# A fused two-model kernel: loads joined and reordered, products evicted in place in PSUM, norm heads reordered, and index products woven with half sweeps

## The chip, the cores and the metric

One core of one Trainium2 chip. The metric is device microseconds of the whole program; lower is better. Everything runs in one launch, with the loads of 250 MB of weights in it.

## What is computed

Two small transformer stacks of two layers each, on 512 tokens of width 1024, in float32, one after the other on the same `x`:

```python
# first_block, l = 0, 1
h = rms(x, norm_g[l]);  proj = h @ w_in[l]
y_a = gla(gq, gk, gv, decay) * silu(gz)                      # gated linear attention
score = sum_h w[t,h] * relu(iq[t,h] . ik[s])                  # 8 index heads of 64
y_b = softmax(q k^T over the top 128 keys of score) v * silu(bz)
y_c = differential attention * silu(cz)
x = x + (sigmoid(g0)*(y_a@w_br0) + sigmoid(g1)*(y_b@w_br1) + sigmoid(g2)*(y_c@w_br2)) @ w_out[l]
# second block, l = 0, 1
h = rms(x, norm1)*(1+scale1) + shift1;  x = x + gate1 * mixer(h @ w_in_2) @ w_out_2
h2 = rms(x, norm2)*(1+scale2) + shift2; x = x + gate2 * (relu(h2 @ w_ff1)**2 @ w_ff2)
```

## The kernel before, in words

**Arithmetic.** Every big product is made of three fp32r matmuls: weights and activations are each split into a high part (rounded to fp32r) and a low part (the rest), and high x high, high x low and low x high are added in PSUM. For a slab of weights `raw` of 128x1024 (two chunks of 128 rows, 512 columns) ScalarE writes the high part `wh` (`high(g)`, L1070), and GpSimd subtracts it from `raw` to give `wl` (L693). SyncE loads the slabs into a ring of `RING`=6 slots; `wh` has `SPLIT`=5. For activations, ScalarE writes `hTh` and VectorE `hTl`.

**The order.** `make_timeline` writes one list, `line`, of steps; every engine walks through that same list and does its own part of each step, in order, so a step's place in `line` is its place in each engine's queue. A *sweep* `(i, p, q)` is what TensorE does with slab q of unit i for a pair p of its four output slices: 2 slices x 2 chunks x 3 matmuls = 12 matmuls (L763). A unit of 1024 rows has 2 pairs x 4 slabs = 8 sweeps, one of 512 rows 4. After a pair's last slab each slice is evicted by `evacuate`, on ScalarE and on VectorE. SyncE and ScalarE do their loads and `high(g)` at the sweep steps, before the eviction; `high` waits both for the slab's DMA and for TensorE's release of the slot.

**PSUM.** Eight banks. Sweeps take banks 0 to 3 in turn (ring `proj`); index products, transposes and small products take 4, 5 and 6 (ring `aux`); a head's transposes take 4 to 7 (ring `turn`). TensorE waits, before it writes a bank, for the event `free` of the bank's last user.

**Scratch.** `scr` has four slots of 128x512, handed out in turn to eviction steps that need a temporary.

**A norm head** (`norm_head`, six of them: the opening, layer 1 of the first block, and two for each layer of the second) turns `x` into `hTh`/`hTl`, pair by pair of the four token tiles: `stats` (ScalarE, squares with a sum, L1184), `scale` (VectorE, a Newton root in 128x1 steps L1592/L1597, then `xn = x * root`, L1602), `turn` (TensorE transposes two half tiles of `xn`, L717; VectorE multiplies by the gain, L1612 or L1617, and adds the shift, L1619, in PSUM; ScalarE copies to `hTh`, L1191; VectorE subtracts to `hTl`, L1626). These steps are laid among the last four sweeps of the unit before and the first four of the unit after.

**The stages that the change touches besides.** The opening: `cf`, four tiles of `x`, twenty small rows (`COLS`), then six slabs, then the late constants in 20 more DMAs. The index stage: 32 products `iq . ik` (L822), four of them for each of the eight sweeps of unit `bk`; ScalarE takes the relu from PSUM to `scr` (L1212) and VectorE adds it, weighted, to `score` (L1668/L1671). The gated branches (`br`), the mixer's output (`mix`), the feed-forward units up (`fu`, L1448, L1450, L1149, L1453) and down (`fd`, L1463, and L1471, L1473, L1477 in the last group). `mod` steps (L1813) are 96 weighted sums of a second stream of weights on VectorE, spread evenly over a list of eligible sweeps; sweeps with a `stats` or `turn` within the next four steps are not eligible.

## Time and profile before

| | |
|---|---|
| runs | 2834.9, 2839.28, 2841.01 us; median 2839.28 |
| the profiled execution | 2836.87 us, of which the span on the core is 2834.8 us |
| TensorE matmul busy | 2523.5 us (89%) |
| VectorE / ScalarE / GpSimd busy | 1439.2 (51%) / 943.5 (33%) / 878.7 us (31%) |
| mean granted TensorE clock | 0.955 of full speed |
| HBM traffic | 249.6 MB read, 90 GB/s over the span |

The busy share of TensorE is that of the whole program. Its idle time is not spread evenly: it lies in the opening, around the norm heads, and in the attention stages, where small operations follow one another from engine to engine.

### The profile page before, as it was taken

To read this page: it belongs to the slowest core of one execution; us is meant where nothing else is said; L and a number is where in the kernel's file an instruction comes from. 1 tells how busy PE (TensorE), PEld (TensorE's weight loads), DVE (VectorE), ACT (ScalarE), POOL (GpSimd) and SP (SyncE) were. 2 spreads that over 40 slices of the span, in tenths; PEclk is the share of its full clock that TensorE was granted. 3 is DMA by queue.
4 is the path that set the end of the run, shared out by engine and by line. 5 is a ranking of instruction groups with operands and counts; after the bars stand their busy time and mean duration, and the time that the engine had idled before them with its cause. 6 is when DMAs were issued, how large, how long until landed. Compare 5 with 4: busy or idle time off the path is not lost. (4 is left out here: it accounts for less than half of the span.)

```text
span 2834.8 us, 34357 instructions
## 1 busy us (share of the span) xinstructions
PE 2523.5 (89%) x12303; PEld 2008.5 (71%) x12303; DVE 1439.2 (51%) x2993; ACT 943.5 (33%) x1695; POOL 878.7 (31%) x366
## 2 busy tenths in 40 slices
PE   5998999889999899989977878999997777899999
PEld 4676877677768677767776547878776644787877
DVE  4496243654368733365465456454556554623334
ACT  3433243432343224342233442322223354232221
POOL 2332314233324242323422002454442200244442
PEclk9999999999999999999998799999998889999999
DMA  4232414134323241313432002444433200233332
GB/s 140 88 90 67 148 39 134 45 97 164 126 65 90 90 141 54 110 58 106 162 88 64 1 1 60 141 162 142 147 121 83 64 1 1 60 95 99 95 96 77
DMA packets 133573, 256.01 MB, mean 90 GB/s; under 512 B 23382, under 2 KB 30116, under 8 KB 133412
## 3 DMA queue, kind: packets, MB, share of 16 engines
q1 hardware_dynamic: 133412, 253.83, 28.5%
q8 instruction: 105, 1.72, 0.2%
q14 instruction: 56, 0.46, 0.1%
HBM read 249.60 MB, written 4.19 MB: 90 GB/s over the span
## 5 line engine op out<-in xcount | busy, mean ns | idle before, releaser
L693 POOL TENSOR_TENSOR wl<-raw,wh 128x1024 fp32r<-128x1024 f32 (+2 forms) x362 | 878.5, 2431 | 1928.5 <-ACT wh L1070 1927.3
L763 PE MATMUL ps<-wh,hTh 128*128 128x512 f32 (+3 forms) x1600 | 645.6, 403 | 16.1 <-DVE hTl L1626 16.1
L1070 ACT ACTIVATE wh<-raw 128x1024 fp32r<-128x1024 f32 (+2 forms) x362 | 379.9, 1049 | 841.4 <-PE ps L763 440.9
L763 PE MATMUL ps<-wl,hTh 128*128 128x512 f32 (+3 forms) x1600 | 625.7, 391 | 0.0
L763 PE MATMUL ps<-wh,hTl 128*128 128x512 f32 (+3 forms) x1600 | 625.2, 391 | 0.0
L763 PEld LDWEIGHTS ps<-wh,hTh 128*128 128x128 f32 x1600 | 311.9, 195 | 86.2 <-issue 30.8
L763 PEld LDWEIGHTS ps<-wh,hTl 128*128 128x128 f32 x1600 | 310.6, 194 | 60.3
L763 PEld LDWEIGHTS ps<-wl,hTh 128*128 128x128 f32 x1600 | 312.1, 195 | 52.7
L763 PE MATMUL ps<-hTh,wh 128*128 128x512 f32 (+2 forms) x704 | 258.8, 368 | 4.9 <-DVE hTl L1626 3.7
L763 PE MATMUL ps<-hTh,wl 128*128 128x512 f32 (+2 forms) x704 | 257.8, 366 | 0.0
L763 PE MATMUL ps<-hTl,wh 128*128 128x512 f32 (+2 forms) x704 | 257.7, 366 | 0.0
L717 PE MATMUL ps<-cf,arena 128*128 128x128 f32 x800 | 133.5, 300 | 136.2 <-DVE arena L1982 23.7
L717 PEld LDWEIGHTS ps<-cf,arena 128*128 128x128 f32 x800 | 101.8, 154 | 175.9 <-issue 82.7
L1813 DVE SCALAR_TENSOR_TENSOR modw<-modw,cact 128x1024 f32<-128x1024 f32 x96 | 151.2, 1581 | 139.9 <-DMA modw<-in_w_mod_dram 139.1
L763 PE MATMUL ps<-wh,yTh 128*128 128x512 f32 x448 | 178.7, 399 | 9.9 <-DVE scr L1450 9.9
L763 PE MATMUL ps<-wl,yTh 128*128 128x512 f32 x448 | 176.0, 393 | 0.0
L763 PE MATMUL ps<-wh,yTl 128*128 128x512 f32 x448 | 175.7, 392 | 0.0
L763 PEld LDWEIGHTS ps<-hTh,wh 128*128 128x128 f32 (+1 forms) x704 | 132.7, 189 | 27.3 <-issue 6.1
L763 PEld LDWEIGHTS ps<-hTh,wl 128*128 128x128 f32 (+1 forms) x704 | 132.7, 189 | 21.3
L763 PEld LDWEIGHTS ps<-hTl,wh 128*128 128x128 f32 (+1 forms) x704 | 132.7, 188 | 21.3
L1448 DVE TENSOR_SCALAR scr<-ps 128x512 f32<-128x512 f32 (+1 forms) x72 | 45.1, 627 | 180.2 <-PE ps L763 180.2
L1463 DVE TENSOR_TENSOR arena<-ps,arena 128x512 f32<-128x512 f32 x96 | 66.3, 691 | 109.3 <-PE ps L763 108.3
(262 smaller groups left out, 3277.1 us busy)
## 6 DMA issues: line engine op xcount, KB each, us to landing
raw<-in_w_in_dram SPq DMA_DIRECT2D x160, 512.0 KB, 3.6
raw<-in_w_ff_dram SPq DMA_DIRECT2D x128, 512.0 KB, 3.7
modw<-in_w_mod_dram SPq DMA_DIRECT2D x96, 512.0 KB, 4.7
raw<-in_w_br_dram SPq DMA_DIRECT2D x24, 512.0 KB, 3.7
raw<-in_w_out_dram SPq DMA_DIRECT2D x24, 512.0 KB, 3.7
xm<-in_x_dram SPq DMA_DIRECT2D x8, 512.0 KB, 4.5
raw<-in_w_out_dram SPq DMA_DIRECT2D x16, 256.0 KB, 3.9
raw<-in_w_in_dram SPq DMA_DIRECT2D x8, 408.0 KB, 3.3
```

The source lines that it names most:

```text
L693: pool.tensor_tensor(piece(wl, g % RING, u), piece(raw, g % RING, u), piece(wh, g % SPLIT, u).bitcast(F32), ALU.subtract)\
L717: last = pe.transpose(dst[:, c * P:(c + 1) * P], src[:, c * P:(c + 1) * P], ident)
L763: last = pe.matmul(*args, start=(q == 0 and c == 0 and n_pass == 0), stop=(q == u["quarters"] - 1 and c == u["chunks"] - 1 and n_pass == 2))
L1070: act.activation(piece(wh, g % SPLIT, u), piece(raw, g % RING, u), ACT.Copy)\
L1448: dve.tensor_scalar(tmp, b, 0.0, None, ALU.max).then_inc(dve_result, mark(dve_result))
L1463: dve.tensor_tensor(acc, b, acc, ALU.add).then_inc(dve_result, mark(dve_result, free))
L1813: dve.scalar_tensor_tensor(w, w, 0.5, cact[:], ALU.mult, ALU.mult, accum_out=modT[:, m // MOD_STEPS, m % MOD_STEPS:m % MOD_STEPS + 1])\
```

## The change

It is a bundle. (1) The opening loads `x` tiles 0 and 1 with a semaphore of their own, then slabs 0 and 1, then `x` tiles 2 and 3, then all small rows as one DMA that the host has laid out, then the other slabs; the late constants are six DMAs. ScalarE makes no `high` before the first `stats`, and writes the opening's squares to `scr`. (2) In every head, ScalarE writes `xn` of the even tile (scale from `nsm[:,3,0:1]`), VectorE that of the odd tile; `stats(0)` and its `scale` stand ahead of the four last sweeps, not behind the first of them; VectorE and ScalarE treat the two tiles of a pair together, first half (`hb`=0) of both, then the second half of both. In the opening, `stats` of pair 1 stand ahead of the first transposes, and two sweeps, not one, ahead of the second ones. (3) `mix`, `br`, `fu`, `fd` and index evictions keep their temporary in the product's own PSUM bank. The bank is freed by the last of the operations. (4) The next-to-last feed-forward group adds the accumulator, scales and adds to `x`, so the last group has two operations a slice and not three. (5) The index stage lays half a sweep (one slice, step `front`, and then the sweep's other slice) behind every two index products, not a sweep behind every four. (6) `logit_max` scales by -q in one 128x1 `tensor_scalar` for each column, where it was one `scalar_tensor_tensor`.

The core of the diff:

```diff
+    def halved(fill):
+
+        return [x for step in fill for x in (("front", *step[1:]), step)]
+
...
-            line.extend(last[0:1] + stats(0) + last[1:3] + two("turn", 0) + last[3:4] + stats(1))
+            line.extend(stats(0) + last[0:3] + two("turn", 0) + last[3:4] + stats(1))
             line.extend(first[0:3] + two("turn", 1) + first[3:4] + then + first[4:])
         else:
-            line.extend(stats(0) + [("columns",)] + two("turn", 0) + stats(1))
-            line.extend(first[0:1] + two("turn", 1) + first[1:4] + [("constants",)] + then + first[4:])
+            line.extend(stats(0) + [("columns",)] + two("stats", 1) + two("turn", 0) + [("scale", stage, 1)])
+            line.extend(first[0:2] + two("turn", 1) + first[2:4] + [("constants",)] + then + first[4:])
 
     if 1 in blocks:
...
-            weave(idx, U("bk", C_BK, 512, tok()))
+            weave(idx, halved(U("bk", C_BK, 512, tok())))
...
+            first_stage = ("n", 0) if 1 in blocks else ("a", 0)
+            for pair, sem in enumerate((first_x_loaded, x_loaded)):
+                for t in (2 * pair, 2 * pair + 1):
+                    sp.dma_start(xm[:, t], a["x"][0, t * P:(t + 1) * P, :]).then_inc(sem, mark(sem, by=16))
+                for t in (2 * pair, 2 * pair + 1):
+                    note(("x", first_stage, t), sem)
+                if pair == 0:
+                    load_weights(0)
+                    load_weights(1)
+            sp.dma_start(rows[0:N_COLS, :], a["rows"]).then_inc(const_loaded, mark(const_loaded, "consts", by=16))
+
...
+                    sp.dma_start(rows3[0:96, :], a["rows_mod"]).then_inc(late_loaded, mark(late_loaded, by=16))
+                    sp.dma_start(rows2[0:64, :], a["rows_pe"]).then_inc(late_loaded, mark(late_loaded, by=16))
+                    sp.dma_start(glag.rearrange("p l n -> p (l n)"), a["gla_gains"].partition_broadcast(P))\
+                        .then_inc(late_loaded, mark(late_loaded, by=16))
+                    sp.dma_start(lqk.rearrange("p k n -> p (k n)"), a["lambdas"].partition_broadcast(P))\
+                        .then_inc(late_loaded, mark(late_loaded, by=16))
...
-                if q == 0:
-                    for s in (2 * p, 2 * p + 1):
+                for k in halves:
+                    mode, idx, c0, n = pair[k]
+                    s = 2 * p + k
+                    if q == 0:
                         bank("proj", ("ps", i, s))
-                for k, (mode, idx, c0, n) in enumerate(pair):
-                    s = 2 * p + k
...
+                if kind == "front":
+                    sweep(*step[1:], halves=(0,))
+                elif kind == "sweep":
+                    sweep(*step[1:], halves=(1,) if ("front", *step[1:]) in fronts else (0, 1))
...
-                    pe.wait_ge(dve_result, at("xn", stage, t))
+                    pe.wait_ge(act_result if t % 2 == 0 else dve_result, at("xn", stage, t))
...
-            for g in range(3):
-                high(g)
-            made = [3]
+            made = [0]
...
-                    act.activation(xn[:, t % 2], xm[:, t], ACT.Square, accum_out=stat[:, 7, t:t + 1])\
+                    if t >= 2 and opening:
+                        act.wait_ge(act_result, at("ss", stage, t - 2))
+                    squared = scr[:, 2 * (t % 2):2 * (t % 2) + 2].rearrange("p a n -> p (a n)") if opening else xn[:, t % 2]
+                    act.activation(squared, xm[:, t], ACT.Square, accum_out=stat[:, 7, t:t + 1])\
                         .then_inc(act_result, mark(act_result, ("ss", stage, t)))
+                    if opening and t % 2 == 1:
+                        for g in range(2):
+                            high(made[0])
+                            made[0] += 1
+                    if opening and t == TILES - 1:
+                        act.wait_ge(act_result, at("ss", stage, t))
+                elif kind == "scale":
+                    _, stage, pair = step
+                    act.wait_ge(dve_result, at("root", step))
+                    act.activation(xn[:, 0], xm[:, 2 * pair], ACT.Copy, scale=nsm[:, 3, 0:1])\
...
+                    for hb in range(2 * (t % 2)):
+                        for t2 in (t - 1, t):
+                            st = ("turn", stage, t2)
+                            act.wait_ge(dve_result, at("h32", st, hb))
+                            act.activation(hTh[:, 4 * hb:4 * hb + 4, t2 * P:(t2 + 1) * P],
+                                           ps[:, bank_of.get((st, hb), 0)].rearrange("p (c n) -> p c n", c=4), ACT.Copy)\
...
-                    act.activation(scratch(("scr", step))[:, 0:WIDTH[t]], ps[:, bank_of.get(step, 0), 0:WIDTH[t]], ACT.Relu)\
-                        .then_inc(act_result, mark(act_result, ("relu", step), ("free", step)))
+                    b = ps[:, bank_of.get(step, 0), 0:WIDTH[t]]
+                    act.activation(b, b, ACT.Relu).then_inc(act_result, mark(act_result, ("relu", step)))
...
+                    dve.tensor_tensor(b, b, grow[:, c * 512:(c + 1) * 512], ALU.mult).then_inc(dve_result, mark(dve_result))
+                    dve.wait_ge(dve_result, now(dve_result))
+                    dve.tensor_tensor(dst, b, dst, ALU.add)\
+                        .then_inc(dve_result, mark(dve_result, free, *([("x", ("f", l), idx)] if c else [])))
...
-                    dve.tensor_tensor(tmp, b, tmp, ALU.mult).then_inc(dve_result, mark(dve_result, ("relu2", i, s), free))
+                    dve.tensor_tensor(b, b, tmp, ALU.mult).then_inc(dve_result, mark(dve_result, ("relu2", i, s), ("free", key)))
                     dve.wait_ge(dve_result, now(dve_result))
                     dve.wait_ge(act_result, at("fh", i, s))
-                    dve.tensor_tensor(F[g % 2][1][:, idx, t0:t0 + n], tmp, F[g % 2][0][:, idx, t0:t0 + n].bitcast(F32), ALU.subtract)\
-                        .then_inc(dve_result, mark(dve_result, ("free", key), *([] if mode == "feat0" else [("f", l, g, idx)])))
+                    dve.tensor_tensor(F[g % 2][1][:, idx, t0:t0 + n], b, F[g % 2][0][:, idx, t0:t0 + n].bitcast(F32), ALU.subtract)\
+                        .then_inc(dve_result, mark(dve_result, free, *([] if mode == "feat0" else [("f", l, g, idx)])))
...
+                    if g == FF_GROUPS - 2:
+                        dve.tensor_tensor(b, b, acc, ALU.add).then_inc(dve_result, mark(dve_result))
+                        dve.wait_ge(dve_result, now(dve_result))
+                    dve.tensor_tensor(b, b, grow2[:, c * 512:(c + 1) * 512], ALU.mult).then_inc(dve_result, mark(dve_result))
...
+                        dve.scalar_tensor_tensor(b, g, 1.0, b, ALU.add, ALU.mult)\
+                            .then_inc(dve_result, mark(dve_result, ("free", gate)))
+                        dve.wait_ge(dve_result, now(dve_result))
+                        dve.tensor_tensor(dst, b, dst, ALU.add).then_inc(dve_result, mark(dve_result, free, *fin))
...
+                    dve.wait_ge(dve_result, at("guess", step, 3, 0))
+                    dve.tensor_scalar(nsm[:, 3, 0:1], y[:, 0:1], -1.0 / 8192.0, None, ALU.mult)\
+                        .then_inc(dve_result, mark(dve_result, ("root", step)))
+                    t = 2 * pair + 1
+                    dve.wait_ge(dve_result, at("guess", step, 3, 1))
+                    dve.tensor_scalar(xn[:, t % 2], xm[:, t], y[:, 1:2], -1.0 / 8192.0, ALU.mult, ALU.mult)\
+                        .then_inc(dve_result, mark(dve_result, ("xn", stage, t)))
...
-                    dve.scalar_tensor_tensor(s[:, 2:2 + k], s[:, 0:k], -1.0, q_scale(m, t, h), ALU.mult, ALU.mult)\
-                        .then_inc(dve_result, mark(dve_result, ("bias", l, m, n)))
+                    for c in range(k):
+                        ins = dve.tensor_scalar(s[:, 2 + c:3 + c], s[:, c:c + 1], -1.0, q_scale(m, t, h)[:, c:c + 1],
+                                                ALU.mult, ALU.mult)
+                    ins.then_inc(dve_result, mark(dve_result, ("bias", l, m, n)))
```

The steps inside `turn` on VectorE are the same operations as before in the new order; `free` of the bank moves with the last of them.

## Rows read from the trace of the kernel before

**Rows 1.** The page, part 1: busy us, share of the span, instructions.

```profile
PE 2523.5 (89%) x12303; PEld 2008.5 (71%) x12303; DVE 1439.2 (51%) x2993; ACT 943.5 (33%) x1695; POOL 878.7 (31%) x366
```

**Rows 2.** Waits of TensorE, whole span: us in total, times, longest us.

```profile
PE ps L763 <- DVE scr L1450: 17.9, 16, 1.7
```

**Rows 3.** Timeline 0 to 70 us: start, us, engine, line, operation, [idle before].

```profile
1.19 1.84 SPq L568 DMA_DIRECT2D xm<-in_x_dram  x4
...
15.87 11.55 POOL L693 TENSOR_TENSOR wl<-raw,wh 128x1024 fp32r<-128x1024 f32 x5 [15.43 <-ACT wh L1070]
...
21.12 1.04 ACT L1184 ACTIVATE arena<-xm 128x1024 f32<-128x1024 f32 x1
...
23.40 1.75 DVE L1583 TENSOR_SCALAR nsm<-stat 128x2 f32<-128x2 f32 x1 [23.40 <-ACT arena L1184]
...
30.98 3.27 PEld L717 LDWEIGHTS ps<-cf,arena 128*128 128x128 f32 x16 [16.63 <-DVE colT L1537]
...
36.13 0.77 PE L763 MATMUL ps<-wh,hTh 128*128 128x512 f32 x1 [1.47 <-DVE hTl L1626]
```

**Rows 4.** The loads of x: from issue to landing.

```profile
DMA to landing us min/median/max: 3.8/6.0/7.8
```

**Rows 5.** Waits of TensorE, 712 to 745 us: head of layer 1.

```profile
PE ps L717 <- DVE arena L1602: 2.8, 1, 2.8
```

**Rows 6.** Waits of TensorE, 1405 to 1440 us: head before the second block.

```profile
PE ps L763 <- DVE hTl L1626: 5.0, 2, 2.8
```

**Rows 7.** Waits of TensorE, 1725 to 1772 us: head before feed-forward, layer 0.

```profile
PE ps L717 <- DVE arena L1602: 7.8, 3, 3.8
PE ps L763 <- DVE hTl L1626: 1.8, 1, 1.8
```

**Rows 8.** Waits of TensorE, 2110 to 2152 us: second block's layer 1.

```profile
PE ps L763 <- DVE hTl L1626: 9.7, 2, 6.9
PE ps L717 <- DVE arena L1602: 2.1, 2, 1.1
```

**Rows 9.** Timelines of VectorE and TensorE, 2780 to 2800 us: feed-forward.

```profile
2785.95 2.40 DVE L1453 TENSOR_TENSOR f2l<-scr,f2h 128x512 fp32r<-128x512 f32 x1 [2.37 <-ACT f2h L1149]
...
2788.99 0.69 DVE L1450 TENSOR_TENSOR scr<-ps,scr 128x512 f32<-128x512 f32 x1
...
2789.89 0.47 PE L763 MATMUL ps<-wh,yTh 128*128 128x512 f32 x1 [0.96 <-DVE scr L1450]
```

**Rows 10.** One line each: duration ns min/median/max, first and last start.

```profile
L1463 DVE TENSOR_TENSOR arena<-ps,arena x96: 683/692/693, 1859.0 to 2806.6; 128x512 f32<-128x512 f32 x96
...
L1507 DVE TENSOR_TENSOR xm<-xm,scr x32: 691/692/2840, 529.8 to 1370.1; 128x512 f32<-128x512 f32 x32
...
L1592 DVE TENSOR_SCALAR nsm<-nsm x72: 260/266/274, 27.5 to 2463.9; 128x1 f32<-128x1 f32 x72
...
L1790 DVE SCALAR_TENSOR_TENSOR soft<-soft,stat x64: 159/161/2105, 355.2 to 1270.7; 128x1 f32<-128x1 f32 x32, 128x2 f32<-128x2 f32 x32
```

**Rows 11.** Timeline of TensorE, 128 to 136 us: index products and sweep.

```profile
128.78 0.50 PE L763 MATMUL ps<-wh,hTh 128*128 128x512 f32 x1
...
131.73 2.93 PE L822 MATMUL ps<-arena 64*128 64x512 f32 x8
134.59 0.50 PE L763 MATMUL ps<-wh,hTh 128*128 128x512 f32 x1
```

**Rows 12.** Timeline of VectorE, 99 to 101 us: the first index sums.

```profile
99.98 0.29 DVE L1668 TENSOR_SCALAR arena<-scr,arena 128x128 f32<-128x128 f32 x1
```

**Rows 13.** Timelines of VectorE and TensorE, 660 to 690 us: merged branches.

```profile
676.95 3.36 DVE L1813 SCALAR_TENSOR_TENSOR modw<-modw,cact 128x1024 f32<-128x1024 f32 x1
...
680.98 1.11 PE L717 MATMUL ps<-cf,xm 128*128 128x128 f32 x4 [5.41 <-DVE hTl L1997]
```

**Rows 14.** Timeline of VectorE, 2826 to 2835 us: the last operations.

```profile
2831.03 0.69 DVE L1477 TENSOR_TENSOR xm<-xm,scr 128x512 f32<-128x512 f32 x1
```

**Rows 15.** Stages: us, busy of each engine (count), PEclk, DMA share, GB/s.

```profile
728.00:732.00 4.00, 3.25 (x17) 3.25 (x17) 3.34 (x5) 2.13 (x3) 1.25 (x2) 0.63 0.36 131
```

155 lines of the change are left out of this document (55 added, 100 removed).

## The prediction, on record before the change was run

> **What bounds the kernel now.** The page comes first: TensorE is busy for 2523.5 of 2834.8 us [rows 1], so the weight products set the time, and VectorE or ScalarE matter only where TensorE waits for them. The waits of TensorE, the second view, are many and short. The single largest is the opening: TensorE's first transposes start at 30.98 us after an idle stretch of 16.6 us and the first sweep at 36.13 [rows 3]. Then come the heads (2.8 us in layer 1 of the first block [rows 5], 5.0 us before the second block [rows 6], 7.8 + 1.8 us before feed-forward [rows 7], 9.7 + 2.1 us in the second block's layer 1 [rows 8]), and 16 waits of up to 1.7 us for a PSUM bank behind the feed-forward eviction, 17.9 us in all [rows 2]. The chain that ended last is no help here: it is 1% of the span, the last products and evictions. The third view, the durations of one line, shows why VectorE is late. An operation with one operand in PSUM takes 683 to 693 ns, 96 times out of 96 (L1463), whereas one with two tensors in SBUF takes 691 at best and up to 2840 ns (L1507) [rows 10]; in the timeline such an operation at 2785.95 took 2.40 us [rows 9]. In the timeline the long ones run while GpSimd subtracts a slab, and they end when it ends. No operation that reads PSUM does so.
>
> **The opening.** The four loads of x go out from 1.19 to 3.0 us and land 3.8 to 7.8 us after issue [rows 3, 4]: tile 0 at about 5.0, tile 3 at about 10.4. The first `stats` starts at 21.12, since five `high` of slabs that come behind twenty small DMAs are ahead of it in ScalarE's queue. After the change tile 1 should be there at about 7 (it is the second of four, 1.8 us apart) and `stats` runs 7.0 to 9.2. VectorE's root took from 23.40 to 29.3, of which 4.0 us were two 128x2 operations, one of them 1.75 us [rows 3], that waited behind GpSimd, who was busy without a break from 15.87 for 11.55 us [rows 3]. After the change GpSimd's first subtraction cannot begin before `high(0)` ends at about 10.4, so these two run free, and the rest of the root are 128x1 forms, which took 260 to 274 ns in all 72 cases [rows 10]: root at 12.0. ScalarE writes `xn` of tile 0 by 13.1 (1.04 us as the square in [rows 3]). TensorE still waits for the joined rows, which are queued behind cf, four tiles and two slabs, 6 x 1.4 us of transfer behind 5.0: 13.5. Transposes 13.9 to 17.5 (16 of them took 3.3 us, at 30.98 [rows 3]). ScalarE has `stats` 2 and 3 and `high(2)`, `high(3)` in front of the copies to `hTh`: 13.2 to 17.6. First sweep at about 19, where it was 36.13: 17 us. What else was in its shadow moves too, because pair 1's root no longer waits for its own `stats`. I take 16; the bounds are 10 (slab 1 or the rows land 3 us later, and `xn` of tile 1 is blocked twice by GpSimd, 2.4 us each [rows 9]) and 18.
>
> **The norm heads.** Per pair, VectorE has 4 gain operations (8 with a shift) and 4 subtractions, about 0.7 us each. Before, the first `hTl` half tile is written after all 8, 6.0 us behind the first transpose; after, it is written after 4, 3.5 us behind. TensorE has 2.0 us of transposes and one sweep of 2.7 us in that time, so the waits for L1626 (the 5.0, 1.8 and 9.7) nearly go. But pair 1 is then late: its `stats` wait for the evictions that VectorE does behind pair 0, and that chain (8.4 us of turn, 1.4 to 2.8 of eviction, 1.2 stats, 2.2 root, 1.05 for ScalarE's `xn` where VectorE needed 0.75) is as long as before. So part of the gain comes back as a wait of 4 to 6 us ahead of the second transposes, long enough that the clock falls: behind the 2.8 us wait of layer 1 the granted clock is 0.63 of full in 728 to 732, so mostly at its lower level of 1.2 GHz [rows 5, 15], which costs about 1.5 us. Head by head: layer 1 of the first block has no second wait, gets 2.8 and the clock: 4.0. Before the second block: 0.95 earlier at the first transposes, 2.7 at the last wait, 0.5 and the clock off: 1.5. Feed-forward, twice: 4.0 and 1.8 earlier, but the chain holds pair 1 (4.2 of it stay), and the first bank wait grows by 1.7, as `fu` keeps its bank for a third operation and VectorE reaches it later: 2.5 each. Second block, layer 1: the six operations of the old last group on two slices, 5 us on VectorE, become four of 0.7, so 7.0. Together 17.5; bounds 6 and 26.
>
> **Feed-forward evictions.** The bank now comes free after max, square, ScalarE's copy and subtraction, not after max and square. In the timeline of the last of 14 transitions the blocked subtraction of slice 2 starts 3.94 us before TensorE goes on and takes 2.40; slice 3's square ends 0.21 before [rows 9]. After: 0.69 for that subtraction (it reads PSUM), then 0.72 + 0.72 + 0.70 for max, square and copy, 0.69 for the second subtraction: end 0.4 before the old point. So each bank wait shrinks by 0.2: 14 x 0.2 = 2.8. This is a cover that just suffices: if the subtraction is blocked after all, each transition loses 1.5 us, 21 in all. Bounds -21 and +5.
>
> **Index stage.** 12 matmuls and 4 products take 134.59 - 128.78 = 5.81 us, of which the four products 2.86 [rows 11]; TensorE waits for nothing in it, so halves can gain nothing there. At 0.227 us a matmul the 12 need 2.72, and the other 0.23 is for changing between the two kinds. Eight more changes a layer cost 16 x 0.23 = 3.7. Further, a bank is now free only after VectorE's sum, and VectorE does its first one at 99.98 [rows 12], since it computes the roots of `bq` first; the fourth product then waits for it, about 1 us in layer 0. Later products have slack: 0.7 product + 0.6 relu + 0.7 sum, against 2.9 us until the ring of three comes round. I take a loss of 4.5; bounds 8 (each of 32 groups waits 0.1 more) and 1.
>
> **Merged branches.** The merge of layer 0 waits 5.41 us for a bank; a `mod` of 3.36 us stands in VectorE's queue in front of the subtraction [rows 13]. `mod` steps are spread over the eligible sweeps, and the new heads make one sweep in each of two heads ineligible (181 become 179), so this `mod` moves one sweep forward. With the `br` sums no longer blocked (up to 2.84 us [rows 10]), the wait falls to about 2.2, and the slow clock behind it goes: 4.5. Bounds 0 and 6.
>
> **Attention, branches, tail.** `logit_max`'s operation takes 160 ns or, blocked, up to 2105 [rows 10]. Two 128x1 forms cost 0.1 to 0.2 more and are never blocked; with the `br` sums I take 2, bounds -2 and +8, since small gains on VectorE reach TensorE only at some of its waits. The end: the last two slices take two operations each, so the last, at 2831.03 [rows 14], ends 1.3 us sooner. `mix` and `fd` only free their banks 0.7 us later, with 8 us of sweeps in between: nothing. The 20 DMAs less on SyncE are part of the opening.
>
> The Trainium skill speaks against (6): its page "SBUF — State Buffer", section "Who interferes with whom", lets `tensor_scalar` take the pair of ports that it shares with GpSimd, whereas a `scalar_tensor_tensor` does so only by its two inputs, so the new form would be blocked as well. The 128x2 form of it in [rows 3] was; the 128x1 forms with a pointer in [rows 10] were not, 72 times of 72. By the skill's page the term would be 0 and not 2.
>
> The Trainium skill, page "VectorE: DVE Perf Modes", section "The TRN2 errata", also gives a PSUM source 62 cycles more than an SBUF one. L1463 with PSUM takes at most 693 ns and L1507 with SBUF alone at least 691 [rows 10], so the trace shows no such surcharge; by the skill's page two operations on the critical eviction would cost 0.13 us more, and the 14 bank waits would shrink by 0.07 and not 0.2, about 2 us less gain.
>
> **The sum.** 16 + 17.5 + 2.8 - 4.5 + 4.5 + 2 + 1.3 = 39.6. From the profiled execution, 2836.9 (span 2834.8 and 2.1 around it), this gives 2797.3; the median of the runs, 2839.3, is 2.4 higher, so 2799 for the median.
>
> **The rivals.** (a) The heads give only what the chain of pair 1 lets through: every head's gain reappears as the wait ahead of its second transposes, and 17.5 becomes 6: 2811. For it: that chain is as long as before. Against: the layer-1 head had no second wait. Chance 0.18. (b) The opening is worth 10: 2805; it is bound by the landing of rows and slabs and by ScalarE's queue. Chance 0.15. (c) Cascades: each operation freed of GpSimd starts the next sooner in the attention stages too, and the heads give 26; 39.6 + 8.5 + 6 = 54: 2785. Chance 0.19. (d) The end on the other side: the index banks. Three banks, held through relu and sum. If that chain were to last longer than the 2.9 us of two products and half a sweep, every one of 32 groups would wait for it. It decides from 1.3 us a group, 32 x 1.3 = 42, more than all gains: at 1.6 us, 51, the time is 2846. It needs a relu from PSUM to PSUM or a sum from PSUM at more than double the 0.6 and 0.7 us; the forms with a PSUM operand speak against it. Chance 0.03. The case of the sum, 2791 to 2808, has 0.45. Faster by over 0.2% (5.7 us, about what a measurement here can tell) in all but (d): 0.94; same 0.03; slower 0.03. The range 2784 to 2815 holds (a), (b) and most of (c).
>
> **What would show it.** First sweep near 19 us and VectorE's 128x2 steps at 0.17; waits for L1626's successor under 1 us, but waits of 4 to 6 us for ScalarE's `xn` ahead of the second transposes of the heads; all subtractions of `fu` at 0.69 and bank waits near 1 us; no waits in the index stage but the first; last operation 1.3 us sooner behind the last product. It is wrong if a subtraction from PSUM is blocked, if index products wait in every group, or if TensorE's opening starts later than 24.

## The result, and the profile after

The changed kernel takes 2767.8 us (median of 4 runs, 2766.95 to 2771.24), beside 2837.8 for the kernel before on the same chip (median of 4, 2834.9 to 2841.01). The ratio is 0.9755, with a 95% interval from 0.9738 to 0.9772: 70 us less. Forecast were 2799 and a range from 2784 to 2815, so the direction was right and the size wrong by 31 us, outside the range on the fast side. The profiled execution has a span of 2766.0 us, against 2834.8.

The page of the changed kernel, part 1 [rows 1 show the same of before]:

```profile
PE 2514.3 (91%) x12303; PEld 2003.8 (72%) x12303; DVE 1373.0 (50%) x3041; ACT 953.3 (34%) x1707; POOL 875.1 (32%) x366
```

TensorE is busy 9 us less and the span is 69 us shorter, so some 60 us are waits that went. VectorE is busy 66 us less, mainly since many of the operations that were stretched while GpSimd subtracted a slab now read PSUM and are not (the `mod` steps still take up to 3.42 us), but that is no measure of the gain, as the experiments show.

Waits of TensorE over the whole span of the changed kernel (us in total, times, longest), those of the norm heads (L1186, L1629), of the merge (L2002), of the feed-forward eviction (L1453) and of the index products (L1217):

```profile
PE ps L706 <- ACT arena L1186: 22.7, 6, 5.8
...
PE ps L706 <- DVE hTl L2002: 3.9, 2, 2.0
PE ps L752 <- DVE hTl L1629: 3.4, 5, 1.1
...
PE ps L752 <- DVE yTl L1453: 1.4, 2, 0.8
...
PE ps L814 <- ACT ps L1217: 0.3, 1, 0.3
```

What the reader is to see is above all what is not there. Of the 17.9 us in 16 waits for the feed-forward eviction [rows 2] only 1.4 us in 2 waits are left, each in the first feed-forward unit of a layer; the 14 transitions of the prediction have none. The waits for the first half tile of `hTl` (5.0, 1.8 and 9.7 us [rows 6 to 8]) are down to 3.4 in all. In their place stand waits for ScalarE's `xn` (L1186), up to 5.8 us ahead of the second transposes, as forecast. The two merges wait 3.9 us together, where the first alone waited 5.41 [rows 13].

The opening, in the timeline of the changed kernel:

```profile
6.82 1.06 ACT L1175 ACTIVATE scr<-xm 128x1024 f32<-128x1024 f32 x1 [4.81 <-DMA xm<-in_x_dram]
...
9.13 0.17 DVE L1582 TENSOR_SCALAR nsm<-stat 128x2 f32<-128x2 f32 x1 [9.13 <-ACT scr L1175]
...
11.56 1.15 ACT L1186 ACTIVATE arena<-xm,nsm 128x1024 f32<-128x1024 f32 x1 [0.66 <-DVE nsm L1599]
...
12.51 0.36 PE L776 MATMUL ps<-cf,arena 64*128 64x64 f32 x1 [12.51 <-DMA arena<-in_rows_dram]
13.28 3.65 PE L706 MATMUL ps<-cf,arena 128*128 128x128 f32 x16 [0.41 <-DVE colT L1536]
...
18.03 0.47 PE L752 MATMUL ps<-wh,hTh 128*128 128x512 f32 x1 [1.11 <-DVE hTl L1629]
```

`stats` begins at 6.82 (forecast 7.0), VectorE's 128x2 step takes 0.17 and not 1.75 us, TensorE waits for the joined rows until 12.51 (forecast 13.5), and the first sweep starts at 18.03 (forecast 19).

Where the 69 us of the span came from is read by laying the same instruction of the two timelines side by side; the gain so far is the difference of their starts:

| up to | start before | start after | gain so far | in this stage | forecast |
|---|---|---|---|---|---|
| opening, to the transpose of the late constants | 51.28 | 31.89 | 19.4 | 19.4 | 16 |
| end of the index stage, layer 0 | 145.03 | 125.78 | 19.3 | -0.1 | -2.3 |
| gla, attention, branches | 580.29 | 562.32 | 18.0 | -1.3 | 1 |
| merge, layer 0 | 685.93 | 662.52 | 23.4 | 5.4 | 4.5 |
| head of layer 1 | 731.89 | 704.12 | 27.8 | 4.4 | 4.0 |
| end of the index stage, layer 1 | 841.92 | 810.80 | 31.1 | 3.3 | -2.3 |
| rest of layer 1, then the second block's head and attention | 1655.82 | 1620.08 | 35.7 | 4.6 | 2.5 |
| mix and feed-forward head, layer 0 | 1760.66 | 1721.61 | 39.1 | 3.3 | 2.5 |
| feed-forward, layer 0, to the next head | 2121.08 | 2070.57 | 50.5 | 11.5 | 1.4 |
| head of layer 1, second block | 2144.85 | 2090.48 | 54.4 | 3.9 | 7.0 |
| its attention and mix, and the last head | 2467.34 | 2407.42 | 59.9 | 5.5 | 2.5 |
| feed-forward, layer 1, to the last product | 2828.50 | 2758.95 | 69.6 | 9.6 | 1.4 |

The two feed-forward stages (21 us, forecast 2.8) and the two index stages (3.2 us gained with what stands ahead of them, forecast 4.5 lost) stand out: 18 and 8 us of the 31 that were missed. How much of the index stages is the granted clock is taken up below.

### The profile page after: what moved, and what is told of

Read it like the earlier page. It is cut to its first block, busy times and chain, and to the rows that moved or that the text cites. A ratio compares the mean times of both kernels' runs of the same rounds, so it can differ in the third digit from the quotient of the medians.

```text
span 2766.0 us, 34344 instructions
## 1 busy us (share of the span) xinstructions
PE 2514.3 (91%) x12303; PEld 2003.8 (72%) x12303; DVE 1373.0 (50%) x3041; ACT 953.3 (34%) x1707; POOL 875.1 (32%) x366
## 4 chain that ended last, share of the span: by engine, by line
PE 74%; DVE 16%; ACT 5%; issue 3%; DMA 1%; SPq 0%; ACTq 0%; DVEq 0%
PE ps L752 60%; PE ps L706 4%; DVE arena L1685 2%; DVE top L1683 2%; PE ps L1041 1%; PE ps L899 1%; PE ps L1002 1%; PE ps L814 1%; PE ps L879 1%; DMA raw<-in_w_out_dram 1%; DMA raw<-in_w_in_dram 1%; PE ps L874 1%; DVE ps L1625 1%; DVE nsm L1399 1%; DVE soft L1960 1%
## 5 line engine op out<-in xcount | busy, mean ns | idle before, releaser
L1463 DVE TENSOR_TENSOR arena<-ps,arena 128x512 f32<-128x512 f32 x80 | 55.2, 690 | 97.3 <-PE ps L752 95.9
```

Source lines behind the costliest of these rows:

```text
L1463: dve.tensor_tensor(acc, b, acc, ALU.add).then_inc(dve_result, mark(dve_result, free))
```

## The experiments

The kernels' expectations speak of 2767.8 us for the changed kernel and 2837.8 for the kernel before; beside the experiments the latter gave medians from 2841.4 to 2847.1, and the changed kernel, run again among them, 2766.6. Those medians of the kernel before lie up to 10 us above 2837.8, so a difference of about 5 us between experiments that did not run side by side is likely at best; where it matters, the ratio to the kernel before beside the run is given (0.9755 and, run again, 0.9736 for the changed kernel). Theories A to G are each set out in the expectation that names them first. Line numbers of an experiment can be off by one to ten from those of the changed kernel.

### Banks or evictions: four kernels

The diff also moved a line: before, a sweep asked for the banks of both its slices ahead of its first matmul; after, each slice asks for its own. The prediction gave that line no price. The first kernel undoes it in the changed kernel:

```diff
-                    if q == 0:
-                        bank("proj", ("ps", i, s))
+                    if q == 0 and k == halves[0]:
+                        for kk in halves:
+                            bank("proj", ("ps", i, 2 * p + kk))
```

> The changed kernel, except that a whole sweep waits for the banks of both its slices before the first matmul, as the kernel before did. Theory A (the 17.9 us of bank waits behind the feed-forward evictions vanished because the second slice's bank is now asked for only 6 matmuls, 1.36 us, after the first's): the waits of TensorE for VectorE's feed-forward eviction come back, 14 to 16 of them at 0.7 to 1.5 us each, 10 to 18 us in all, and the time is 12 to 20 us above the changed kernel's 2767.8 (2780 to 2788). Theory B (they vanished because the eviction's subtraction reads PSUM and is no longer blocked by GpSimd): no bank waits in the feed-forward stage, and the time stays within 3 us of 2767.8.

Measured: 2789.1 us, 21 slower. Its waits of TensorE:

```profile
PE ps L753 <- DVE yTl L1454: 8.9, 8, 1.6
...
PE ps L753 <- DVE f2l L1454: 6.7, 8, 1.3
```

All 16 bank waits are back, 15.6 us, though every subtraction is as short as in the changed kernel (at most 0.69 us). Theory A holds; the time is 1 us above its range. Second, the same edit alone in the kernel before:

```diff
-                if q == 0:
-                    for s in (2 * p, 2 * p + 1):
-                        bank("proj", ("ps", i, s))
...
+                    if q == 0:
+                        bank("proj", ("ps", i, s))
```

> The kernel before, with one edit: each slice of a sweep asks for its bank just before its own first matmul. Theory A: the 16 bank waits (17.9 us) for L1450 go, a few more behind other evictions shrink, and the time falls by 15 to 22 us from 2837.8, to 2816 to 2823. Theory B: the evictions are as before, so at most the second bank of each pair is hidden; the first one is still late and the waits stay above 12 us: 2832 to 2838.

Measured: 2824.5, ratio 0.9927 (0.9901 to 0.9953), 17 us faster, and the waits for L1450 are down from 17.9 to 0.4 us in 2, with the old evictions and their long subtractions (up to 2.61 us). Third, the changed kernel with the old form of the eviction (ScalarE's copy and the subtraction, not shown, read `tmp` too):

```diff
-                    dve.tensor_tensor(b, b, tmp, ALU.mult)...("relu2", i, s), ("free", key)
+                    dve.tensor_tensor(tmp, b, tmp, ALU.mult)...("relu2", i, s), free
```

> The changed kernel with the feed-forward eviction of the kernel before: the square goes to the SBUF scratch, ScalarE's copy and the subtraction read the scratch, and the bank is free after the square. Theory A: the bank is free earlier, not later, so no bank wait appears; the subtractions are blocked by GpSimd again (up to 2.8 us), which costs at most the first sweeps of fd: within 3 us of 2767.8. Theory B: the waits of up to 1.7 us for the bank come back, 10 to 18 us: 2778 to 2788.

Measured: 2773.3, by the medians 5.5 slower, at a ratio of 0.9753, which is that of the changed kernel; 0.8 us of bank waits in 3 places, and subtractions of up to 2.79 us. Theory B, which wanted 10 to 18 us of waits, is excluded. Fourth, the new eviction alone in the kernel before (the third edit, the other way round):

> The kernel before with the changed feed-forward eviction alone (square, copy and subtraction in PSUM, bank free after the subtraction), both banks of a sweep still asked for together. Prediction's term: 16 bank waits shrink by 0.2 us each, 3 us faster, 2835. Theory A: the same, between 4 us faster and 6 us slower (the bank is held for a copy and a subtraction longer). Theory B: the bank waits go, 12 to 18 us faster: 2820 to 2826.

Measured: 2838.9 against 2841.8 of the kernel before (10 and 14 runs), ratio 0.9993 (0.9975 to 1.0011): nothing that can be told in the time, and theory B is excluded. Its waits of TensorE, however, show both sides of the new eviction:

```profile
PE ps L763 <- DVE yTl L1453: 9.8, 8, 3.1
...
PE ps L763 <- DVE f2l L1453: 7.1, 8, 1.5
```

The 14 waits that the prediction counted take 12.2 us where they took 16.7 in the kernel before (windows from 1800 to 2110 and from 2500 to 2820 us in both traces), 0.3 us less each. The first one of each layer, which stands in the head, took 0.6 us twice and takes 1.6 and 3.1: the bank is held longer there. So the shorter wait of the prediction was real, and its other side took most of it back.

### The index stage: three kernels

The changed kernel with whole sweeps beside the index products, sums still in PSUM:

```diff
-            weave(idx, halved(U("bk", C_BK, 512, tok())))
+            weave(idx, U("bk", C_BK, 512, tok()))
```

> The changed kernel with whole sweeps beside the index products again, one for every four products; relu and sum still in PSUM. The prediction's theory (each change between the two kinds of matmul costs 0.23 us, 16 more of them cost 3.7 us, and halves gain nothing): 3 to 4 us faster than 2767.8, and both index stages (small turn to first key turn) near 48 us. Theory C (TensorE takes the index products faster when only two stand in a row; layer 1's stage went from 50.7 to 46.9 us): the stage of layer 1 is back at 50.7, and the decay wait behind it shrinks by 1.8, so the kernel is 2 to 5 us slower.

Measured: 2788.6, 21 slower, far beyond both. Its waits of TensorE:

```profile
PE ps L814 <- DVE arena L1671: 11.3, 8, 4.0
...
PE ps L814 <- DVE arena L1674: 5.4, 8, 0.8
```

Four products in a row against three banks that are held through relu and sum: TensorE waits for VectorE in each of the 16 groups, 16.7 us. So the bank mechanism of the prediction's rival (d) is real, and the halves are what keeps it away. Next, the other half of the edit undone: halves kept, relu into SBUF.

```diff
-                    act.activation(b, b, ACT.Relu).then_inc(..., ("relu", step))
+                    act.activation(scratch(("scr", step))[:, 0:WIDTH[t]], ps[...], ACT.Relu)...("free", step)
```

> The changed kernel with the index relu written to the SBUF scratch and summed from there, as before; the halved sweeps are kept. Theory C: layer 1's index stage stays near 47 us, since the halves make it shorter: within 2 us of 2767.8. Theory D (the shorter stage comes from relu and sum in PSUM, and no longer from blocked VectorE sums): the stage is back near 50.7 us, and VectorE's sums take up to 2 us when GpSimd is at work; 2 to 5 us slower. The prediction's bank term (sum in PSUM holds the bank longer, 1 us): 1 us faster.

Measured: 2762.8 (2760.9 to 2765.1), ratio 0.9704 (0.9678 to 0.9731): by the medians 4 to 5 us faster than the changed kernel, more than the 1 us of the bank term. The changed kernel, run again later, had 0.9736 (0.9715 to 0.9758); the intervals overlap, so this is likely and not settled. And both parts undone, which is the index stage of before in the changed kernel:

> The changed kernel with the whole index edit undone: relu into SBUF, and whole sweeps, one for every four products. Theory G (four products in a row wait for the third bank, whose relu stands behind a high in ScalarE's queue: 0.66 us on the weight-load row, while two products in a row never do): the index stages take 50.7 us again in layer 1, TensorE's waits for the relu on the weight-load row come back at 3 to 5 us a layer, and the kernel is 4 to 9 us slower than the one with relu in SBUF and halves (2762.8): 2767 to 2772. The prediction's theory (a change of kind costs 0.23 us, halves gain nothing): 7 us faster than 2762.8, 2756.

Measured: 2772.3, 9.5 slower than with halves and the relu in SBUF, and by the medians 4.5 slower than the changed kernel. Its ratio of 0.9757 (0.9727 to 0.9787) is only 0.0002 to 0.0021 above that of the changed kernel, so the whole index edit is worth between nothing and 6 us by the times; of the loss of 4.5 that the prediction had, nothing is seen. The reason is in the trace of the kernel before, on a row that the prediction passed over. Waits of the kernel before in the index stage of layer 0 (95 to 146 us), and in its timeline one of the eight:

```profile
PEld ps L822 <- ACT scr L1212: 4.1, 8, 0.7
```

```profile
132.89 1.57 ACT L1212 ACTIVATE scr<-ps 128x512 f32<-128x512 f32 x3
...
133.54 0.29 PEld L822 LDWEIGHTS ps<-arena 64*128 64x128 f32 x2 [0.66 <-ACT scr L1212]
```

The weight load of the fourth product waits 0.66 us for a bank, since ScalarE had a `high` of 1.06 us in front of the first relu. The matmul row hides it: it says 2.93 us for eight matmuls (two a product), without a wait. With the index edit undone the row is back, in the stage of layer 1 (763 to 814 us):

```profile
PEld ps L814 <- ACT scr L1216: 4.1, 8, 0.7
```

The timeline of the changed kernel:

```profile
113.01 1.13 PE L814 MATMUL ps<-arena 64*128 64x512 f32 x4
...
114.07 0.50 PE L752 MATMUL ps<-wh,hTh 128*128 128x512 f32 x1
...
115.66 1.13 PE L814 MATMUL ps<-arena 64*128 64x512 f32 x4
```

Two products take 1.06 us (114.07 - 113.01), four in a row took 2.86 [rows 11]. Six matmuls of a half with the changes of kind take 1.59 (115.66 - 114.07), twelve took 2.95. So four products and twelve matmuls take 2 x (1.06 + 1.59) = 5.30 us and not 5.81. The 0.23 us for each further change of kind is there as forecast; 0.74 went, of which 0.66 is the wait. Not all groups are this wide, so eight times 0.51, 4.1 us a layer, is an estimate from above. The cleanest measure is the stage of layer 1 (small turn to first key turn) with whole sweeps and the relu in SBUF, and then in the changed kernel, at nearly the same granted clock (us, busy of each engine, PEclk, DMA share, GB/s):

```profile
763.50:813.40 49.90, 47.43 (x188) 30.90 (x189) 31.37 (x70) 20.48 (x45) 10.43 (x5) 0.97 0.15 45
```

```profile
763.80:810.80 47.00, 44.94 (x188) 27.72 (x189) 26.94 (x70) 20.19 (x45) 10.47 (x5) 0.96 0.16 49
```

That is 49.8 and 46.9 us: the edit gives 2.9 in this layer. In the kernel before the stage took 50.7 at a granted clock of 0.94, so about 0.9 of those 3.8 us are the clock.

In layer 0 the same stage took 49.8 us before and 49.9 after. The granted clock differs there. The stretch at the start of the stage, in the changed kernel and then in the kernel before:

```profile
76.00:92.00 16.00, 15.71 (x59) 10.26 (x59) 8.04 (x28) 2.66 (x11) 0.74 (x1) 0.70 0.10 39
```

```profile
95.00:107.00 12.00, 11.59 (x51) 8.47 (x52) 7.45 (x27) 2.79 (x13) 1.05 (x1) 0.86 0.16 64
```

At a mean of 0.70, TensorE is at the lower level, 1.2 GHz, in some 60% of these 16 us, and in 28% of the 12 us before; both lie behind the 2.7 us wait for the small turn that both kernels have. An estimate from these shares is 3 us lost to the clock, as much as the edit gives. How long the slow part lasts differs from one execution to the next: the changed kernel, run again, has a mean clock of 0.93 in both of its index stages, where this profile has 0.90 and 0.96. Whether the change makes it longer on the average was not tried.

### The norm heads: six kernels

The order of the evictions, by which the prediction wanted the waits for `hTl` (5.0, 1.8 and 9.7 us) to go, put back (per tile, four subtractions behind all gains):

```diff
-                    for hb in range(2 * (t % 2)):
-                        for t2 in (t - 1, t):
...
+                    for hb in range(2):
+                        act.wait_ge(dve_result, at("h32", step, hb))
...
```

> The changed kernel with the head's evictions in the old order on ScalarE and VectorE: per tile both halves, and the four subtractions behind all gains. Prediction (VectorE's first half tile is then there 2.1 to 2.5 us later in each of the six heads, and the second transposes are late anyway because pair 1's stats wait for the evictions): waits for hTl of 2 to 9 us come back ahead of the first sweeps, 15 to 18 us in all, and the waits for ScalarE's xn (22.7 us now) shrink or grow by the chain of pair 1; net 8 to 16 us slower (2776 to 2784). Rival (the chain of pair 1 lets only 6 us through in all): 3 to 6 us slower.

Measured: 2767.4, no difference, and less than either expectation. The waits have only changed places: 18.1 us for `hTl` in 7 (3.4 in 5 in the changed kernel), and 5.2 for `xn` in 3 (22.7 in 6). Next, `xn` of a pair's first tile:

```diff
-                    pe.wait_ge(act_result if t % 2 == 0 else dve_result, at("xn", stage, t))
+                    pe.wait_ge(act_result if t % 2 == 0 and stage == first_head else dve_result, at("xn", stage, t))
```

> The changed kernel with xn of a pair's first tile written by VectorE again in all heads but the first. Prediction (ScalarE's 1.05 us against VectorE's 0.75, and no third engine in the chain): the waits of 4.4 to 5.8 us ahead of the second transposes shrink by 0.2 to 0.4 us each: 0 to 2 us faster. Rival (VectorE's subtraction-free form is blocked by GpSimd in some of the heads, up to 2.8 us): those waits grow by 1 to 2 us each where it is, 2 to 8 us slower.

Measured: 2770.5 (2768.6 to 2778.2), 3 to 4 us slower, less than its own runs scatter; the two theories are not told apart. The third part of the edit is one step in a list:

```diff
-            line.extend(stats(0) + last[0:3] + two("turn", 0) + last[3:4] + stats(1))
+            line.extend(last[0:1] + stats(0) + last[1:3] + two("turn", 0) + last[3:4] + stats(1))
```

> The changed kernel with one step of the head put back: the stats of pair 0 stand behind the first of the last four sweeps, not ahead of it. For VectorE and ScalarE they come one sweep (2.7 us) later in the queue, behind that sweep's high. Theory E (this move, and not the order of the evictions, is what the heads gained, because xn of pair 0 is ready when the first transposes come): waits of 1 to 2.8 us come back ahead of the first transposes of layer 1's head and of the feed-forward heads, 4 to 8 us slower (2772 to 2776). The prediction put 0.5 to 0.95 us on it at the head before the second block and nothing elsewhere: within 2 us of 2767.8.

Measured: 2787.9, 20 us slower, far beyond both. All three parts together:

> The changed kernel with all three edits of the five inner heads undone: stats one sweep later, xn of both tiles on VectorE, evictions tile by tile. Prediction (the heads are worth 17.5): 2785. Rival (a) of the prediction (the chain of pair 1 lets only 6 us through): 2774. The sum of what the single edits have shown so far (evictions 0, xn on VectorE 3 slower) and of theory E (4 to 8): 2774 to 2779.

Measured: 2786.7, 19 us. So the three parts are together worth 19 us, near the 17.5 that were forecast for the heads, and nearly all of it is the stats, one sweep earlier. But this step also moves 47 of the 96 `mod` steps, through the list of sweeps beside which they may stand. Two kernels part the two: in one only the `mod` places are put back (the test for `stats` looks at 4 steps, not 5), in the other only the stats (the test for `stats` and `turn` looks at 6).

> The changed kernel with the mod steps beside the same sweeps as in the kernel before. The step of the head that moves the stats also takes one more sweep in two heads out of the list beside which mod steps may stand (179 for 181), and so 47 of the 96 mod steps stand one listed sweep earlier; putting the stats back (20 us slower) put these back too. Theory E (the stats cost it): this kernel is within 3 us of 2767.8. Theory F (the mod steps' places cost it): the wait ahead of the first merge is back near 5.4 us, other waits behind late evictions grow too, and the time is 8 to 15 us above 2767.8.

> The changed kernel with the stats of pair 0 one sweep later in the inner heads, and the mod steps kept beside the sweeps of the changed kernel. Theory E: as with the stats put back alone, 15 to 20 us above 2767.8. Theory F: only the waits ahead of the first transposes of the heads (8.7 us more in the trace with the stats put back): 5 to 12 us above 2767.8, and this and the other kernel's loss add up to the 20.

> The changed kernel itself, beside the others on the same chip: 2765 to 2771. It gives the scatter against which the small differences (ScalarE's xn, branch sums, evictions tile by tile, index in SBUF) are read.

Measured: mods put back 2774.2 (2771.3 to 2777.9), stats put back 2785.6 (2784.9 to 2786.6), the changed kernel beside them 2766.6 (2762.7 to 2773.3). The stats cost 19 us by themselves. The `mod` places cost about 7 by the medians, with intervals that overlap (0.9739 to 0.9776, and 0.9715 to 0.9758), and the two do not add up: with both put back the loss is 20. The wait ahead of the first merge did not come back with the `mod` places (3.9 us in 2 as before), so that part of theory F is wrong. The waits for `xn` with the stats one sweep later and `mod` kept:

```profile
PE ps L706 <- ACT arena L1186: 30.5, 11, 5.9
```

Five waits more than the six above, 7.8 us: those ahead of the first transposes. TensorE's idle time grows by 13.6 us in all (245.0 to 258.6, the sums of the idle times on its matmul rows), and it is busy 5.3 us more (2519.6 for 2514.3).

### The opening, the branch sums, and two kernels more

The joined rows in 20 small DMAs at the same place of SyncE's queue:

```diff
-            sp.dma_start(rows[0:N_COLS, :], a["rows"])...
+            for lo, hi in zip(cuts, cuts[1:]):
+                sp.dma_start(rows[lo:hi, :], a["rows"][lo:hi, :])...
```

> The changed kernel with the joined rows fetched by 20 small DMAs at the same place of the queue (the same bytes from the joined array). If TensorE's start at 12.5 us is set by the landing of the rows, it goes out by 20 issues of 0.4 to 0.6 us less one, 8 to 11 us later, to 21 to 23, and slabs 2 to 5 come as much later; the time is 6 to 10 us above 2767.8. If small DMAs overlap and only the order in the queue counts, 0 to 3 us.

Measured: 2771.9, by the medians 4 us slower, at a ratio of 0.9756, so not clear of noise. TensorE starts at 16.19 and not at 12.51, 3.7 later. Part of that is scatter: in the other traces with the opening unchanged it starts between 12.2 and 13.8, so the twenty small DMAs cost 2.4 to 4.0 us. Their issues take 7.06 us of SyncE's queue, and slabs 2 to 5 go out at 11.48 where it was 5.48. TensorE's start came earlier than the 21 to 23 that were expected. By elimination most of the opening's 19.4 us is therefore the order in the queues; its parts were not tried one by one. The branch sums in SBUF again:

```diff
-                        dve.scalar_tensor_tensor(b, g, 1.0, b, ALU.add, ALU.mult)...
-                        dve.tensor_tensor(dst, b, dst, ALU.add)...
+                        dve.scalar_tensor_tensor(g, g, 1.0, b, ALU.add, ALU.mult)...
+                        dve.tensor_tensor(dst, dst, g, ALU.add)...
```

> The changed kernel with the branch sums in the old form: gate times product into the SBUF gate, then the sum of two SBUF tiles (up to 2.84 us where GpSimd is at work); the bank is free one operation earlier. Prediction (the 3.4 us that the wait ahead of the first merge lost came mostly from here, and some of the 2 us of attention and branches): that wait is back at 4 to 5 us, and the time 3 to 5 us above 2767.8. Rival (banks are asked for slice by slice now, so what VectorE does behind a branch is hidden, and the wait fell because the mod step moved): within 1 us.

Measured: 2773.9, with two runs at 2765.1 and 2768.0 and a granted clock of 0.953 to 0.954, and two at 2779.7 and 2781.3 and 0.949 to 0.950: unclear. In its trace the waits ahead of the two merges are 6.2 us in all, the longest 4.1 (3.9 and 2.0 in the changed kernel), so a part of the merge's gain does come from here.

The kernel before with the two edits that proved large, banks by slice and stats one sweep earlier (both shown above, the other way round):

> The kernel before with two edits only: banks asked for slice by slice (alone: 17.4 us faster, 2824.5), and the stats of pair 0 one sweep earlier in the inner heads (with the mod steps' places that follow from it). If what the undoing of it cost in the changed kernel (18 to 20 us) is its worth by itself: 2804 to 2808. If it needs the new order of evictions in the head to be worth something (the wait for hTl, 19.8 us, stands behind it and takes it up): 2812 to 2824.

Measured: 2796.2, ratio 0.9834 (0.9806 to 0.9862), 46 us faster than the kernel before and below both expectations. Beside the 17 us of the banks alone the stats (and the `mod` places) bring 28 here by the medians, where they cost 18 to 20 when undone in the changed kernel; the two intervals together leave some 10 us either way, so it is open whether this is more. Its waits of TensorE:

```profile
PE ps L717 <- DVE arena L1601: 7.7, 5, 2.4
```

This was 23.1 us in 12 waits in the kernel before. The wait for `hTl` grows only from 19.8 to 22.4.

Last, a try at more: relu in SBUF, and halves also beside the attentions, `weave(attention("b"), halved(...))` and `weave(attention("c"), halved(branch(1)))`.

> A try at a better kernel: the changed kernel with the index relu in SBUF (2762.8) and, further, with halved sweeps also beside the two attentions of the first block. If TensorE's waits there (5.8, 4.2 and 2.2 us at prob turns and masks) come from work standing in lumps, halves spread it and take 3 to 8 us off, to 2755 to 2760; if they come from VectorE's chain of softmax steps, as their releasers say, it costs the changes between the kinds of matmul, 32 sweeps x 0.23 = 7 us a layer at most, and nothing is gained: 2763 to 2777.

Measured: 2763.4, with runs from 2753.6 to 2769.0. In its trace the first block ends 13 us sooner than in the changed kernel. The second block then gives all of it back, in code that is the same: over its attention steps the granted clock was 0.70 where it was 0.85 in the changed kernel (this kernel, then the changed one):

```profile
1530.00:1580.00 50.00, 40.69 (x216) 23.91 (x216) 25.60 (x91) 21.82 (x71) 0.00 (x0) 0.70 0.00 1
```

```profile
1540.00:1585.00 45.00, 34.81 (x222) 20.26 (x218) 26.91 (x95) 22.94 (x76) 0.00 (x0) 0.85 0.00 1
```

The profile is of the slowest of its four runs. Two runs had a mean granted clock of 0.948 and 0.949 over the whole program and took 2769.0 and 2768.7 us; the other two had 0.956 and 0.957 and took 2758.2 and 2753.6. So the clock here differs between executions of one kernel, and what the halves beside the attentions are worth at an equal clock is hidden by it: an estimate from the profile is that 0.948 for 0.954 cost some 17 us (2767 x 0.052 less 2766 x 0.046). By the median it is no better than relu in SBUF alone. That kernel, 2762.8, is the best median that is shown here.

## Why the prediction was wrong

**Banks.** The step that failed is "So each bank wait shrinks by 0.2: 14 x 0.2 = 2.8. This is a cover that just suffices". The arithmetic of the eviction was about right (0.3 us less for each of the 14 waits in the kernel before with the new eviction alone); what it was held against was not. It let TensorE go on when both banks are free, as before. After the change the first slice's bank is enough, and the second's is asked for six matmuls later, 1.36 us (6 x 0.227). [rows 9] show it: slice 2 was squared, and its bank free, before 2785.95, 3.94 us ahead of TensorE's start; only slice 3's was late, by 0.96, less than 1.36. In the changed kernel, at the same place:

```profile
2717.50 0.69 DVE L1453 TENSOR_TENSOR f2l<-ps,f2h 128x512 fp32r<-128x512 f32 x1 [2.21 <-ACT f2h L1139]
...
2720.30 0.69 DVE L1453 TENSOR_TENSOR f2l<-ps,f2h 128x512 fp32r<-128x512 f32 x1 [0.78 <-ACT f2h L1139]
```

```profile
2720.46 0.39 PE L752 MATMUL ps<-wh,yTh 128*128 128x512 f32 x1
...
2721.82 0.39 PE L752 MATMUL ps<-wh,yTh 128*128 128x512 f32 x1
```

The pair starts at 2720.46 on slice 2's bank, free at 2718.19. Slice 3's is free at 2720.99, 0.53 after the start, and wanted at 2721.82: 0.83 to spare. With both asked for at once this would be a wait of 0.5, and the kernel with the pair put back has 0.52 at its last transition. Undone, this one line costs 21 us; alone it gives 17. The term stood at 2.8 and had no price for the line at all; the eviction that it did price shows no gain in the time when it is alone, since the first wait of each layer grows.

**Index.** "TensorE waits for nothing in it, so halves can gain nothing there" was read from the matmul rows alone. The waits for a bank stand on the weight-load rows, 4.1 us a layer. The 0.23 us for a change of kind was right. Instead of 4.5 lost, the edit gives up to 6 us (4.5 by the medians, 2.9 in the stage of layer 1 alone), and likely more with the relu in SBUF.

**Heads.** The size came out near, 17.5 against 19 with all three parts undone, but by luck: the 17.5 hold 7.0 that the prediction gave to the shorter last feed-forward group, which none of these kernels undoes, and that head gained 3.9. The order of the evictions, on which the prediction built, is worth nothing (2767.4 without it), just as rival (a) said for that part: pair 1's chain takes back what the first sweep gains. The stats one sweep earlier had no term of their own, and cost 19 us when put back. In the trace 7.8 of it are waits ahead of the first transposes, 5.8 other waits, and 5.3 more busy time at the same work, that is a lower granted clock (0.952 for 0.954). Why the other waits and the clock follow was not tried.

**The opening** was right step by step to about 1 us. The 16 that was taken was lower than the 17 that the steps gave; 19.4 came. **Merge:** 5.41 became 2.02 (forecast 2.2), gain 5.4 for 4.5; but it is 2.0 with the `mod` step in its old place too, so only the branch sums are seen to matter (4.1 with them in the old form), and what brought the rest is not shown. **The end:** the last sum ends 1.96 us behind the start of the last matmul where it was 3.22, the 1.3 of the forecast. That the span ends 5.1 us after it in this profile, and 3.1 in that of the kernel before, is scatter of the last store: it is 3.1 when the changed kernel is run again. **Blocked operations:** the term rested on the 128x1 forms never being blocked. The 96 steps of the new form took:

```profile
L1794 DVE TENSOR_SCALAR soft<-soft,stat x96: 203/214/218, 339.8 to 1241.6; 128x1 f32<-128x1 f32 x96
```

None was blocked, though 28 of them ran while GpSimd was subtracting a slab, where the form before took up to 2105 ns [rows 10]. Their worth in us was not tried alone. The prediction read more out of the Trainium skill ("SBUF — State Buffer", "Who interferes with whom") than stands there: by that section a `tensor_scalar` can be held up only when its operands allow the mode with two ports, and it makes no statement on a single element per partition. The traces fit that: the 128x2 form took up to 2261 ns and the 128x1 forms never more than 274 [rows 10]. No feed-forward subtraction from PSUM took more than 0.69 us, these among them:

```profile
L1453 DVE TENSOR_TENSOR f2l<-ps,f2h x32: 690/691/693, 1756.3 to 2720.3; 128x512 fp32r<-128x512 f32 x32
```

The Trainium skill's surcharge for a PSUM source ("VectorE: DVE Perf Modes", "The TRN2 errata") does not show after the change either: at most 693 ns with PSUM, at least 691 without [rows 10].

So the 31 us are about 18 (banks), 8 (index, of which the clock and what stands ahead of the stages are a part), and 5 net of smaller terms, some above and some below their forecast; 2 of these are the step from the profiled execution to the median, which the sum added to the kernel before and the changed kernel did not show. No run undoes the shorter last group (4) or the in-place evictions of `mix` alone. No rival held the time: (c), at 2785, was the nearest, and it was thought to come from cascades, which were not it.

## What to carry to other kernels

Ask for a resource where it is first used and not where the group begins: one line that splits the wait for two banks was worth 17 to 21 us here, more than all the faster evictions that were to end the same wait. Read the weight-load rows for TensorE's waits, as well as the matmul rows. When a long chain feeds a stage, as here a norm head, starting it one sweep earlier can count for more than the order at its end. Where a diff moves one line in passing, that line wants a price of its own.

## What the runs showed of the hardware

The granted clock of the same code differs from one execution to the next. The changed kernel had mean clocks of 0.90 and 0.96 in its two index stages in one profile, and 0.93 and 0.93 in the other. Four runs of the last kernel had 0.948, 0.949, 0.956 and 0.957 over the whole program and took 2769.0, 2768.7, 2758.2 and 2753.6 us. So a gain that is seen in one stage of one profile need not arrive at the end, and a difference of 10 us between two profiles is to be held against their clocks first.

A `tensor_scalar` of 128x1 on VectorE was never stretched (96 of at most 218 ns, 28 of them while GpSimd was at work), while in the kernel before the small `scalar_tensor_tensor` (128x1 and 128x2) took up to 2105 ns and a `tensor_scalar` of 128x2 up to 2261.

A wait of TensorE for a PSUM bank can stand on the weight-load row alone: 8 times up to 0.7 us in an index stage, with none on the matmul row. Twenty small DMAs in place of one delayed TensorE's start by 2.4 to 4.0 us, and the next loads by 6.0; their issues took 0.35 us each.
